# Two block transformer kernel: the sums of the second modulation one place later, and a token-wise value projection partly run by weight tile

## What is computed

```python
for i in range(DEPTH_2):
    shift_x, scale_x, gate_x = jnp.split(sc @ w_mod[i] + b_mod[i], 3, axis=-1)
    shift_c, scale_c, gate_c = jnp.split(sctx @ w_mod[i] + b_mod[i], 3, axis=-1)
    hx = modulate(rms_norm_2(x, norm_g[i]), shift_x[:, None], scale_x[:, None])
    hc = modulate(rms_norm_2(ctx, norm_g[i]), shift_c, scale_c)
    # i == 0: diff_attention_mixer, q, k, v, g = split(h @ a_w_in)
    # i == 1: window_gqa_mixer,     q, k, v, g = split(h @ b_w_in), 4 key and value heads of 64
    x = x + gate_x[:, None] * (ox @ w_o[i])
```

## Time and profile before

| | |
|---|---|
| runs, us | 2988.46, 2987.06, 2983.96 |
| profiled execution, us | 2984.43 |
| its span, us | 2982.6 |
| granted clock of TensorE, mean | 0.98 |
| busy: TensorE / its weight loads / DVE / ACT / POOL | 95% / 80% / 59% / 33% / 35% |

### The profile page before, as it was taken

How to read it: one execution, slowest core, us unless ns; L and a number is a source line. 1 busy time by engine, 2 the same in 40 slices (tenths; PEclk the granted TensorE clock), 3 DMA queues, 4 the chain that set the end, 5 groups by cost and what they waited for, 6 DMA issues and landing times. The chain is left out here.

```text
span 2982.6 us, 42609 instructions
## 1 busy us (share of the span) xinstructions
PE 2823.3 (95%) x16380; PEld 2378.5 (80%) x16380; DVE 1759.4 (59%) x2531; ACT 991.3 (33%) x1746; POOL 1029.5 (35%) x635
## 2 busy tenths in 40 slices
PE   7899999999999999999989998899989898999998
PEld 6778787778888888778878888888878687878876
DVE  4743453665555545567776438888853594077853
ACT  4122561311111111141111217777750201177731
POOL 2323214654444455332322221333343163211231
PEclk9899999999999999999999999999999899999998
DMA  5544521111111111123344412221111132442111
GB/s 188 196 156 141 130 68 47 50 50 56 49 49 42 42 49 49 35 65 126 141 164 155 146 67 96 72 89 54 63 33 41 35 135 102 123 124 55 30 43 71
DMA packets 214037, 255.63 MB, mean 86 GB/s; under 512 B 9385, under 2 KB 182638, under 8 KB 213886
## 3 DMA queue, kind: packets, MB, share of 16 engines
q1 hardware_dynamic: 198306, 190.14, 21.3%
q10 hardware_dynamic: 15584, 63.51, 5.4%
HBM read 188.02 MB, written 65.60 MB: 85 GB/s over the span
## 5 line engine op out<-in xcount | busy, mean ns | idle before, releaser
L1124 PE MATMUL ps<-hh,w_parts 128*128 128x512 f32 (+2 forms) x2320 | 870.0, 380 | 10.4 <-POOL w_parts L875 2.5
L1125 PE MATMUL ps<-hl,w_parts 128*128 128x512 f32 (+2 forms) x2320 | 863.1, 378 | 0.0
L875 POOL TENSOR_TENSOR w_parts<-w_raw,zero 128x1024 fp32r<-128x1024 f32 x132 | 263.5, 1996 | 839.3 <-PE ps L1130 594.3
L1130 PE MATMUL ps<-hh,w_parts 128*128 128x512 f32 (+2 forms) x2320 | 517.0, 377 | 0.0
L1124 PEld LDWEIGHTS ps<-hh,w_parts 128*128 128x128 f32 x2320 | 438.6, 189 | 95.5 <-issue 6.2
L1125 PEld LDWEIGHTS ps<-hl,w_parts 128*128 128x128 f32 x2320 | 438.5, 189 | 82.0 <-issue 0.2
L1130 PEld LDWEIGHTS ps<-hh,w_parts 128*128 128x128 f32 x2320 | 414.9, 188 | 80.0
L877 POOL TENSOR_TENSOR w_parts<-w_raw,w_parts 128x1024 fp32r<-128x1024 f32 x132 | 327.0, 2477 | 10.4
L2064 ACT ACTIVATE f_y<-f_z,convv 128x1024 f32<-128x1024 f32 x44 | 54.8, 1245 | 508.6 <-DVE f_z L2622 508.4
L2812 DVE TENSOR_SCALAR_CACHE_REDUCE b_s<-ps 128x640 f32<-128x640 f32 (+1 forms) x128 | 100.6, 786 | 103.1 <-PE ps L1686 100.0
L2624 DVE SCALAR_TENSOR_TENSOR f_y<-f_z,convv,f_y 128x1023 f32<-128x1023 f32 x44 | 105.1, 2389 | 81.7 <-ACT f_y L2064 81.7
(11 more groups left out here) (380 smaller groups left out, 5288.8 us busy)
## 6 DMA issues: line engine op xcount, KB each, us to landing
w_mod_sb<-in_w_mod SPq DMA_DIRECT2D x16, 1536.0 KB, 8.0
w_raw<-in_w_up SPq DMA_DIRECT2D x44, 512.0 KB, 3.8
w_raw<-in_a_w_in SPq DMA_DIRECT2D x32, 512.0 KB, 4.2
d_raw<-in_w_down SPq DMA_DIRECT2D x22, 512.0 KB, 4.1
w_raw<-in_w_in SPq DMA_DIRECT2D x20, 512.0 KB, 6.0
za_parts<-z_hi ACTq DMA_DIRECT2D x16, 640.0 KB, 3.0
za_parts<-z_lo ACTq DMA_DIRECT2D x16, 640.0 KB, 4.1
d_even<-za_parts SPq DMA_DIRECT2D x16, 640.0 KB, 7.1
```

The source lines that it names most:

```text
L875: pool.tensor_tensor(wh[:, s], w_raw[:, s], zero[:].broadcast_to([P, KT * P]), ALU.add).then_inc(w_high[s], 1)
L1124: pe.matmul(acc[s][:, p0:p0 + w], wh[:, s, wk], hh[:, k, c0:c0 + w], start=(k == 0), stop=False)
L1125: pe.matmul(acc[s][:, p0:p0 + w], wh[:, s, wk], hl[:, k, c0:c0 + w], start=False, stop=False)
L1130: last = pe.matmul(acc[s][:, p0:p0 + w], wl[:, s, wk], hh[:, k, c0:c0 + w], start=False, stop=(k == KT - 1))
```

## The change

In `project_turned` the sums of group n-2 stand behind value tile n. In `project_gates` the sums of group 6 stand behind the first gate tile and those of group 7 behind the second. DVE keeps each group when it empties the accumulator that now holds it, and the gains of the modulation are made after the second gate tile. In `project_by_token`, token tiles 0 to 2 are computed first with weight tile 0 alone, then with weight tile 1 alone, and only the second part waits for the split of weight tile 1; token tiles 3 to 8 are computed with both at once, as before; token tile 9 is computed with tile 0 and then tile 1, and each half releases its weight slot. A half is, for each k, a product of `hh` with 256 columns and one of `hl` with 128. SP's, POOL's and ACT's programs are as before.

```diff
@@ project_turned @@
                 if n:
                     turn_v(pe, n - 1, (n - 1) % 2)
-                    mod_sums_within(pe, (n - 1) // 2, (n - 1) % 2, n % 2)
+                if n >= 2:
+                    mod_sums_within(pe, (n - 2) // 2, n % 2, n % 2)
@@ project_gates @@
             turn_v(pe, 7, 1)
-            mod_sums_within(pe, 3, 1, 0)
+            mod_sums_within(pe, 3, 0, 0)
             project_tile(pe, name, 0, 1, SHIFTED_SEGS)
+            mod_sums_within(pe, 3, 1, 1)
             pe.wait_ge(v_copied, 24)
             norm_columns(pe, "fin", x_sum)
@@ project_by_token @@
             parts = w_parts[:, :, 1:3]
+
+            def half_tile(t, s):
+                tok = slice(t * P, (t + 1) * P)
+                got = bank(t % 5).rearrange("p (s w n) -> p s w n", s=2, w=2)
+                for k in range(KT):
+                    wk = slice(k * P, (k + 1) * P)
+                    pe.matmul(got[:, s], hh[:, k, tok], parts[:, s, :, wk], start=(k == 0), stop=False)
+                    last = pe.matmul(got[:, s, 0], hl[:, k, tok], parts[:, s, 0, wk], start=False, stop=(k == KT - 1))
+                return last
+
             for s in range(2):
                 pe.wait_ge(acc_free[s], A0[name][s] + 1)
+            for s in range(2):
                 pe.wait_ge(w_split[s], W0[name][s] + 1 + 1)
-            for t in range(TOK // P):
+                for t in range(3):
+                    last = half_tile(t, s)
+                    if s:
+                        last.then_inc(v_turned, 1)
+            for t in range(3, TOK // P):
                 if t >= 5:
                     pe.wait_ge(acc_free[(t - 5) % 2], A0[name][(t - 5) % 2] + (t - 5) // 2 + 1 + 1)
+                if t == TOK // P - 1:
+                    for s in range(2):
+                        half_tile(t, s).then_inc(w_used[s], 1)
+                    continue
@@ scale_turned @@
-                scale_tile(dve, name, n // 2, n % 2, divmod(n - 1, 2) if n else None)
+                scale_tile(dve, name, n // 2, n % 2, divmod(n - 2, 2) if n >= 2 else None)
@@ scale_gates @@
-                scale_tile(dve, name, n // 2, s, (3, 1) if n == 0 else None)
-                if n == 0:
+                scale_tile(dve, name, n // 2, s, (3, n) if n < 2 else None)
+                if n == 1:
                     modulate_gains(dve, 1)
-                if n == 1:
```

More of the change, by code:

```diff
@@ L1241, in project_by_token @@
                         pe.matmul(got[:, :, 0], hl[:, k, tok], parts[:, :, 0, wk], start=False, stop=False)
[L1242 to L1246, removed]
+                    last = pe.matmul(got, hh[:, k, tok], parts[:, :, :, wk], start=(k == 0), stop=(k == KT - 1))
                     if k < KT - 1:
                         pe.matmul(got[:, :, 0], hl[:, k, tok], parts[:, :, 0, wk], start=False, stop=False)
-                if t < TOK // P - 1:
-                    last.then_inc(v_turned, 1)
+                last.then_inc(v_turned, 1)
         def project_held(pe, name, segs, held, between):
```

## The result

The changed kernel is slower: 2998.28 us (median of 6 runs, 2996.17 to 2998.63) against 2986.02 for the kernel before in the same sessions (6 runs, 2983.96 to 2990.3). The ratio is 1.0039, with a 95% interval from 1.0028 to 1.0051. The forecast was 2998.0, in a range from 2990.5 to 3003.

A forecast was written before the change was run, and what follows sets the result against it. TensorE, busy 95% of the span, was taken as the bound. Terms -0.1 + 13.8 + 2.3 - 5.1 gave +10.9 us on the profiled 2984.43, so 2995.3; with the median 2.6 us above, 2998.0, range 2990.5 to 3003.

The forecast's parts named there:

- The first gap: Before value tile 2: the 8.75 us gap stays, as 10.5 us ended by POOL; net 0.1 us gained.
- SP's release: At L800, SP's wait for the last sums passes 15.3 us later, moving the first head's loads to about 1693.5.
- The landing: Third gate tile's weights land 12.4 us after SP's release (4.2 MB at 342 GB/s); TensorE loses 13.8 us.
- The clock behind the gap: Behind the third gate tile's gap TensorE restarts at the lower clock level, costing 2.3 us.
- The projection: Token-wise value projection: earlier start, half tiles of 1.84 us and a clock that stays up gain 5.1 us.
- The sum: Whole kernel: -0.1 + 13.8 + 2.3 - 5.1 = +10.9 us.
- (a): Rival at the third gate tile: engines serve its weights between the head's loads; sum +5 us, 2992; chance 0.12.
- (b): Rival at L800: SP's wait passes without the last group, leaving the projection's gain: -5.2 us, 2981.9; chance 0.05.
- (c): Rival at the token-wise projection: it gains nothing; +16 us, 3003; chance 0.07.
- (d): Rival before value tile 2: the 8.75 us gap goes, needing weights at 1546; held excluded, no chance given.

The follow-up runs named there:

- x6: Changed kernel with third and fourth gate weight tiles issued before SP's wait, and value weight pairs one step earlier: ratio 0.9965 to the kernel before.
- x7: Kernel before, sums and projection unchanged, with only the load order of x6: ratio 1.0028.
- x4: Kernel before; SP alone also waits until TensorE has used the second gate weight tile before issuing the first head's loads: ratio 1.0053.
- x1: Kernel before with the changed token-wise value projection alone, sums as before: ratio 0.9981.
- x9: As x6, but DVE empties the second value tile before the first group's modulation steps: ratio 0.9947 to the kernel before.
- x10: As x9, with the norm's column sums and what depends on them one gate tile later: ratio 0.9951 to the kernel before.
- x2: Kernel before with the later sums alone, projection as before: ratio 1.0043.
- x5: Changed kernel; SP issues the third and fourth gate weight tiles before its wait for the last sums: ratio 0.9994 to the kernel before.
- x3: Changed kernel with the last group's sums back behind the first gate tile, other sums late: ratio 0.9991 to the kernel before.
- x8: As x6, with the projection's last token tile computed whole: ratio 0.9972 to the kernel before.

## Why the prediction was right

The mechanism was the one forecast: SP's queue, held one tile longer by the last sums, delays the weights of the third gate tile, and the projection gives back a quarter of it. The terms came out as follows.

**The first gap.** As forecast: POOL ends it. The start is 0.3 us earlier than before, where 0.84 was forecast, and the lower clock behind it takes that back. Net 0 against 0.1 gained. x6 and x7 together show both of its causes.

**SP's release.** Forecast 15.3 us later. It was issued at 1693.65 against 1678.16, 15.5, of which 0.16 belongs to the shift before the stage. x4 shows that this one time can carry the loss.

**The landing.** Here a term was mis-sized: 12.4 us forecast, 13.49 measured. The bytes were right (4.21 MB), the rate was not:

```profile
1693.60:1695.00 1.40, 1.40 (x13) 0.82 0.26 51
1695.00:1707.20 12.20, 0.90 (x5) 0.50 1.01 339
```

From 1695 on the traffic ran at 339 GB/s, as in the earlier trace rows, but in the first 1.4 us it was 51. In the kernel before it was 406 GB/s from 1678.0 to 1679.4, while the store of the value rows, issued at 1677.23, was under way, so that its mean held no start. The time before a queue's first bytes belongs in such a sum beside bytes over rate.
The Trainium skill's page "DMA: Bandwidth & Descriptors" (section "Anatomy of one DMA — SWDGE (gpsimd) path") gives a transfer that GpSimd issues a fixed cost of about 2 us and puts most of it behind the last byte. The loads here are SP's, another path, and the trace shows 1.4 us of near silence at the start; what lies behind the last byte it doesn't separate.

With it TensorE lost 15.0 us (15.12 less 0.16) instead of 13.8.

**The clock behind the gap.** Forecast 2.3 us. From the column sums' successor to the spreading of the norm the two traces part from 15.12 to 17.76 us (L1325 at 1725.90 against L1309 at 1708.14): 2.6. The model for it was a little small: 30.35 us in the prediction is the time to the start of the last row, which has two records, so the ten tiles lost 2.3 to 2.4 us there and not 2.1. How long TensorE worked before the clock rose was 4.0 us behind the first gap, where 5 was assumed, and 5.8 us behind the gap at the gate (by the windows, 1557.37 to 1561.4 and 1709.18 to 1715.0).

**The projection.** Half tiles were forecast at 1.84 us, from the rows of such a pair, and took 1.85; columns alone would have given 1.41. The profile shows weight loads busy for all 11.00 us from 2500 to 2511, in the half tiles, and for 13.97 of 16 us from 2511 to 2527, in the whole ones. So the load of the stationary operand is the likely limit of a half; no run varies it. The gain was 4.65 us instead of 5.1. The missing 0.4 is at the end: DVE's last addition ended at 2532.69 and TensorE began at 2533.21, where I had allowed under 0.1 us, because in the earlier trace rows that wait was not the last one. The window of the earlier trace rows puts the fall of the clock in the old gap at 2485.6 and not at about 2485; the rest of 1.37 us is shorter than either.

**The sum.** The steps add up to +13.0 us (15.0 + 2.6 - 4.65) against a forecast of +10.9. The profiled executions differ by 11.7 and the medians by 12.3. About 1.5 us of the difference comes back in the windowed attention and behind it, where both run the same program. The first to the last context score product there is 249.3 us in the kernel before, 247.4 in the changed one, and between 246.7 and 250.2 in the ten experiments. I call it scatter and don't explain it. So the closeness of 2998.0 to 2998.28 is luck: the terms erred by 2.1 us in sum. 0.7 of that is missing in the difference of the medians (12.3 against 13.0), and 1.0 was the median that I added to (2987.06, where the six runs have 2986.02).

Of the rivals, (a), short landing, fell with the 13.49 us; (b), an early pass of SP, with 53.1 us at L800; (c) with x1; (d) with the 10.85 us gap, and x6 shows the order of loads that it would have needed.

## What to carry to other kernels

Before you move a step, look up every semaphore that it increments and read each queue that waits for it past the wait: here a sum that nobody needed soon held four loads, and behind them the weights that TensorE needed in 14 us. A gap whose releaser is named can have a second cause that ends a few us later; see when that one is ready before you count the gap as gained. And once the critical resource is fed in time, the two fastest kernels of this study (x9 and x10, 0.9947 and 0.9951 of before) came from the same late sums that had cost 12 us.

## What was not expected of the hardware

TensorE's granted clock fell to 0.50 with the engine busy in every window, behind 28 one-column products in a row. It did so in the traces of the changed kernel, x2, x5, x6 and x9, and behind 24 in x3 (0.64 from 1682 to 1684, then 0.50), but not in x8, with the same 28. Behind the 16 column sums alone it fell in x1 (0.50 from 1698 to 1700) and stayed at 1.00 in the kernel before, x3, x7 and x10. What decides is open. And a weight load that comes earlier can slow others down: POOL's split, begun while DVE split a tile, stretched DVE's two operations from 0.83 and 1.49 us to 2.40 and 3.57 (x7).
